# A two-layer attention and retention trunk on one core: in each half chunk of the first MLP product and of the retention q/k product, the low weights' matmul runs one K tile behind the high weights' matmul

## What is computed

```python
def reference(x, norm_mix_g, norm_mlp_g, a_w_qkv, a_q_gain, a_k_gain, a_w_o, r_w_in, r_w_out, mlp_w1, mlp_w2):
    pos = jnp.arange(x.shape[1], dtype=jnp.int32)
    for i in range(DEPTH):
        h = rms_norm(x, norm_mix_g[i])
        if i % N_MIXERS == 0:
            j = i // N_MIXERS
            x = x + moba_mixer(h, a_w_qkv[j], a_q_gain[j], a_k_gain[j], a_w_o[j], pos)
        else:
            j = i // N_MIXERS
            x = x + retention_mixer(h, r_w_in[j], r_w_out[j], pos)
        x = x + sqrelu_mlp(rms_norm(x, norm_mlp_g[i]), mlp_w1[i], mlp_w2[i])
    return x
...
def sqrelu_mlp(h, w1, w2):
    return jnp.square(jax.nn.relu(h @ w1)) @ w2
```

## Time and profile before

| | |
|---|---|
| median of 3 executions | 668.26 us (668.18 to 668.57) |
| the profiled execution | 666.6 us |
| its span, first to last instruction | 664.5 us |
| outside the span | 2.1 us |
| TensorE matmuls busy | 659.0 us, 99% |
| VectorE busy | 423.5 us, 64% |
| ScalarE busy | 332.8 us, 50% |
| granted TensorE clock | 1.000 of full speed |

### The profile page before, as it was taken

The page is one execution under the profiler, slowest core; times in us unless marked ns, Lnnn a source line. Parts: engine busy times, 40 slices in busy tenths (PEclk is TensorE's granted clock), DMA queues, the critical chain, the costliest instruction groups (busy, mean ns, idle before and its releaser), DMA issues.

```text
span 664.5 us, 8894 instructions
## 1 busy us (share of the span) xinstructions
PE 659.0 (99%) x3296; PEld 556.9 (84%) x3296; DVE 423.5 (64%) x469; ACT 332.8 (50%) x435; POOL 26.8 (4%) x29
## 2 busy tenths in 40 slices
PE   8999999999999999999999999999999999999998
PEld 7888888888888888888888888888888888888887
DVE  6898566877776454459975555654578777744541
ACT  7877655655554334364446545454365555533320
POOL 0163000000000000000000000000000000000000
PEclk9999999999999999999999999999999999999999
DMA  9965458566555555535664555456637665565500
GB/s 326 387 222 182 138 168 280 163 197 188 200 187 204 190 190 189 191 127 191 194 226 151 161 164 180 127 181 184 203 108 219 189 187 188 188 208 197 196 1 32
DMA packets 82125, 123.00 MB, mean 185 GB/s; under 512 B 2352, under 2 KB 43824, under 8 KB 82096
## 3 DMA queue, kind: packets, MB, share of 16 engines
q1 hardware_dynamic: 81808, 121.28, 56.0%
q0 software_dynamic: 288, 1.31, 0.5%
HBM read 121.54 MB, written 1.05 MB: 184 GB/s over the span
## 4 chain that ended last, share of the span: by engine, by line
PE 97%; DVE 2%; ACT 1%; issue 0%; DVEq 0%; ACTq 0%
PE acc L585 22%; PE acc L489 18%; PE acc L491 18%; PE acc L490 18%; PE acc L588 11%; DVE lo L1004 1%; ACT hi L773 1%; PE acc L612 1%; PE acc L533 1%; PE scr L491 1%; PE scr L490 1%; PE scr L489 1%; PE acc L536 1%; PE acc L542 1%; PE scr L625 1%; PE scr L718 1%
## 5 line engine op out<-in xcount | busy, mean ns | idle before, releaser
L1004 DVE TENSOR_TENSOR lo<-raw,hi 128x2048 fp32r<-128x2048 f32 x108 | 247.4, 2291 | 118.5 <-ACT hi L773 118.4
L773 ACT ACTIVATE hi<-raw 128x2048 fp32r<-128x2048 f32 x108 | 207.1, 1919 | 129.8 <-PE acc L491 127.7
L585 PE MATMUL acc<-h_both,hi 128*128 128x512 f32 x640 | 222.3, 393 | 0.0
L588 PE MATMUL acc<-h_both,lo 128*128 128x256 f32 x640 | 177.7, 278 | 0.0
L585 PEld LDWEIGHTS acc<-h_both,hi 128*128 128x128 f32 x640 | 119.9, 187 | 27.4
L588 PEld LDWEIGHTS acc<-h_both,lo 128*128 128x128 f32 x640 | 120.3, 188 | 0.0
L489 PE MATMUL acc<-hi,aT_hi 128*128 128x512 f32 x252 | 98.1, 389 | 0.0
L491 PE MATMUL acc<-hi,aT_lo 128*128 128x512 f32 x252 | 98.1, 389 | 0.0
L490 PE MATMUL acc<-lo,aT_hi 128*128 128x512 f32 x252 | 98.0, 389 | 0.0
L489 PE MATMUL acc<-hi,h_both 128*128 128x512 f32 x208 | 83.6, 402 | 0.0
L491 PE MATMUL acc<-hi,h_both 128*128 128x512 f32 x208 | 81.2, 391 | 0.0
(11 more groups left out here) (130 smaller groups left out, 586.5 us busy)
## 6 DMA issues: line engine op xcount, KB each, us to landing
raw<-in_mlp_w SPq DMA_DIRECT2D x64, 1024.0 KB, 5.4
raw<-in_r_w_in SPq DMA_DIRECT2D x24, 1024.0 KB, 5.1
raw<-in_a_w_qkv SPq DMA_DIRECT2D x8, 1024.0 KB, 9.7
raw<-in_r_w_out SPq DMA_DIRECT2D x8, 1024.0 KB, 5.0
raw<-in_a_w_qkv SPq DMA_DIRECT2D x16, 256.0 KB, 6.2
raw<-in_a_w_o SPq DMA_DIRECT2D x4, 1024.0 KB, 5.0
x<-in_x SPq DMA_DIRECT2D x1, 1024.0 KB, 12.0
decay_sb<-in_decay POOLq DMA_DIRECT2D x1, 768.0 KB, 6.5
```

The costliest lines, as they stand in the source:

```text
L585: nc.tensor.matmul(bank, feat_view(hi, s)[:, kt, o * P:(o + 1) * P], h_both[:, kt, :, :].rearrange("p b t -> p (b t)"), start=kt == 0, sto ...
L588: m = nc.tensor.matmul(bank[:, 0:SEQ], feat_view(lo, s)[:, kt, o * P:(o + 1) * P], hT_hi[:, kt, :], start=False, stop=kt == KD - 1)
L773: nc.scalar.activation(hi[:, s, :], raw[:, s, :], ACT.Copy).then_inc(hi_ready, 1)
L1004: nc.vector.tensor_tensor(lo[:, s, :], raw[:, s, :], hi[:, s, :].bitcast(F32), ALU.subtract).then_inc(lo_ready, 1)
```

## The change

Only `wide_feature_form` is changed. The loop over K tiles makes one more turn, and in turn `kt` it issues the wide matmul of K tile `kt` and then the narrow matmul of K tile `kt - 1`. The number of instructions, their shapes, operands and banks are as before, and so are `start` on the first matmul of a half chunk and `stop` on its last. `used` is still counted by the last narrow matmul of the chunk.

```diff
                 pe.wait_ge(acc_free, bank0 + 2)
                 for o in range(2):
                     bank = acc[:, 2 * (s % 2) + o, :]
-                    for kt in range(KD):
-                        if hT_need is not None and o == 0:
-                            pe.wait_ge(hT_ready, hT_need + kt + 1)
-                        nc.tensor.matmul(bank, feat_view(hi, s)[:, kt, o * P:(o + 1) * P],
-                                         h_both[:, kt, :, :].rearrange("p b t -> p (b t)"),
-                                         start=kt == 0, stop=False)
-                        m = nc.tensor.matmul(bank[:, 0:SEQ], feat_view(lo, s)[:, kt, o * P:(o + 1) * P],
-                                             hT_hi[:, kt, :], start=False, stop=kt == KD - 1)
+                    for kt in range(KD + 1):
+                        if kt < KD:
+                            if hT_need is not None and o == 0:
+                                pe.wait_ge(hT_ready, hT_need + kt + 1)
+                            nc.tensor.matmul(bank, feat_view(hi, s)[:, kt, o * P:(o + 1) * P],
+                                             h_both[:, kt, :, :].rearrange("p b t -> p (b t)"),
+                                             start=kt == 0, stop=False)
+                        if kt > 0:
+                            m = nc.tensor.matmul(bank[:, 0:SEQ], feat_view(lo, s)[:, kt - 1, o * P:(o + 1) * P],
+                                                 hT_hi[:, kt - 1, :], start=False, stop=kt == KD)
                 m.then_inc(used, 1)
```

## The result

The changed kernel takes 670.58 us (median of 6, 670.46 to 670.97) against 668.22 us (median of 6, 667.80 to 671.48): ratio 1.0037, 95% interval 1.0021 to 1.0054. It is 0.4% slower, where no change was forecast, and above the range given. The profiled execution took 670.63 us.

What follows compares the result with a forecast made beforehand. The prediction took TensorE's matmul queue to bound the kernel. Exchanged steps summed to -0.02 us and the entry waits to nothing, so the 668.26 us median would stay at 668.3 us, range 667.4 to 669.2.

Steps and rivals of the forecast that it cites:

- What bounds the kernel: Whole kernel: TensorE's matmuls cover 659.0 of 664.5 us, so any matmul cost goes one for one into the time.
- The prices at the seam: Border between half chunks: one 346.7 ns pair becomes 226.5 ns wide-wide plus 120 ns narrow-narrow, 80 times, -0.02 us.
- dear end: Upper bound for the wide-wide step at half chunk borders: 230 ns, giving at most +0.3 us over 80 half chunks.
- faster rival: Pairs inside half chunks: the lag saves about 4 ns in each of 560 steps, 2.2 us, 666.0 us; chance 0.04.
- slower rival: Last narrow matmul of each half chunk: unhidden weight load makes its step 190 ns, +5.6 us, 673.9 us; chance 0.05.
- The waits at the entries: First half chunks' waits on `hT_ready`, about 0.12 us earlier: costed at nothing, at most 0.4 us for three entries.
- The time forecast for the kernel before: Baseline of the sum: profiled execution 666.6 us, span 664.5; the median of 668.26 us was expected to stay.

Runs made afterwards that it cites:

- e6: Kernel before with all 8 wide matmuls of each half chunk issued first, then all 8 narrow ones; 670.33 us, ratio 1.0041.
- e3: Kernel before, but the narrow matmul uses the low weights of K tile kt - 1 with activation tile kt (one term wrong); one profiled execution, 668.88 us.
- before_again: The kernel before, unedited, profiled and timed once more against itself; 667.12 us, ratio 0.9984.
- e8: Kernel before, strictly alternating, with narrow matmuls taking K tile kt - 1 (turn 0: tile 7) except in each stage's first half chunk; 667.40 us, ratio 0.9998.
- e10: Kernel before with wide 7 moved ahead of narrow 6 in the first half chunk of each stage only; 671.38 us, ratio 1.0048.
- after_again: The changed kernel, unedited, profiled and timed once more against the kernel before; 670.81 us, ratio 1.0047.
- e1: Changed kernel, but the narrow matmul streams the activation tile kt just streamed by the wide one (one term wrong); one profiled execution, 671.19 us.
- e2: Kernel before, but the narrow matmul streams activation tile kt - 1 (one term wrong); one profiled execution, 667.42 us.

## Why the prediction was wrong

**What bounds the kernel** was right: the waits and the other engines did not change, and what TensorE needed more went into the time.

**The prices at the seam** (226.5 ns wide to wide, 120 ns narrow to narrow, in sum -0.02 us) were taken for the whole cost of the change, and that is the step that failed. Their own error is small. In the changed kernel the step from wide to wide takes 233 to 236 ns, above the dear end of 230, since behind a narrow matmul the price of the token form is reached only some steps later (e6). The step from narrow to narrow is 113 or 120 ns. The two together average 350.8 ns over the 77 seams inside the stages: 4.3 ns over the forecast, 80 x 4.3 = 0.3 us. The other 3.4 of the 3.7 us are in the 560 pairs that the change doesn't touch, 6.0 ns each, and the prediction put these at nothing. It did so on the sentence "each matmul appears to cost its own fixed time (about 227 ns wide, 120 ns narrow) whoever its neighbour is". e3, `before_again` and e8 show the same alternating instructions at 347 and at 353 ns a pair in one execution, and e10 shows that a swap of neighbours decides it for hundreds of matmuls behind it. The price of a matmul in this stream depends on what went on before it, and a sum of exchanged steps can't hold it. The prediction compared 80 pairs of exchanged steps; it had to ask as well what the other 560 pairs would do. (Its faster rival did ask it, and had the sign the other way.)

In the changed kernel the seams come every 2.8 us and lead each half chunk into the slow rhythm, whichever way the stage was entered: `after_again` entered layer 1 in the fast one (its first half chunk took 2857 ns, those of the two other stages 2904 and 2905) and ran at 2816 to 2822 ns behind the first seam. Layer 1 of e1 did the same. The profile of the result alone couldn't have shown it: there all three stages were already entered in the slow rhythm, by a first step of 316 ns. What keeps the stream slow across each seam, step by step, isn't known.

**The slower rival** had the sign but not the mechanism. It wanted 190 ns for the step between the last two narrow matmuls of a half chunk; that step is 113 or 120 ns: a load does fit behind a narrow matmul, also when another narrow one follows. With this agrees the estimate of 107 ns from the Trainium skill (TensorE: Matmul & The Clock Gate, "LDWEIGHTS (loading the stationary operand)"), though no run here measures what a load itself takes. **The faster rival** is refuted by e2, where the narrow matmul streams another tile than its predecessor and the pair still takes 347 ns, and by e8, where its weights are shifted too.

**The waits at the entries** were costed at nothing, and rightly: the list of waits of TensorE's matmuls has no line of `h_both`, and in `after_again` the first half chunk of layer 1, entered in the fast rhythm, took 2857 ns as those of the kernel before do (2856 to 2863). e6, which advances the wide matmuls by several narrow ones, shows what that margin is worth once it is used up, and that the weight load is what waits.

**The time forecast for the kernel before** hid something too. The prediction made its sum against the profiled 666.6 us and took the median of 668.26 for the same thing with a constant added. The 1.7 us between them can be partly the start, since the feature form begins anywhere from 112.6 to 113.6 us in the profiles here, and partly, in executions like that of `before_again`, a stage in the slow rhythm (the three timed executions have no profile that would tell): 0.8 us for q/k, and by e3 and e8 1.7 us for an MLP stage (its 256 pairs take 90.53 us there against 88.83). So the kernel before already pays some of this loss in some executions. That fits the measured difference of medians, 2.4 us (3.0 for `after_again`), being smaller than the 3.7 us between the two profiles.

## What to carry to other kernels

On an engine that is 99% busy, an exchange of neighbours can't be priced by the exchanged steps alone. Look also at the steps that stay, and compare them over whole stages and between executions of the same kernel: a duration or a start-to-start step with two values for the same line, stage by stage, says that the stream has more than one rhythm. Where a kernel's executions scatter by more than its edits are worth, profile the unchanged kernel several times before explaining an edit by one profile of each. And where wide and narrow matmuls alternate, every irregular place (an entry, a seam, a swap) is a place where the rhythm can change.

## What the runs showed of the hardware that was not expected

- With fp32r operands, equal matmuls in a row take 226.5 ns for 512 columns and 120 ns for 256, at the full granted clock. So 256 more columns cost 106.5 ns, and by that rate 13.5 ns of either step are not for columns (an estimate). An alternation takes the sum of the two (346.7 ns a pair) or 6.6 ns more (353.3).
- Both rhythms keep going for all 31 half chunks behind the first one of an MLP stage, 86 us in the fast and 88 us in the slow one. Of the 24 entries in the profiles whose first half chunk begins in strict alternation, the first step (wide to narrow, behind the transposes) was 312 to 314 ns in the 19 that went on fast and 316 ns in the 5 that went on slow. The nine entries of the lagged order (the changed kernel twice, and e1) agree: 316 ns in the seven that began slow, 313 ns in the two that stayed fast up to the first seam. So it goes with a few ns in how the stream starts. What sets these ns, and what inside TensorE keeps the two rhythms apart, is open: the profile has no view of it, and no kernel here was built to tell.
- A run of narrow matmuls leaves its trace in about the next five wide steps (233, 236, 228, 233, 231 ns, then 227), while the other way round only the first narrow step is odd (113 ns).
